# Per-head normalisation of the new vectors moved to VectorE, and their turns one step later, in a one-core decoder layer

## The reference

```python
h = rms_norm(x, attn_norm[i])
(mq, mk, mv, nsq, kc, vc, ksl, vsl, kwn, vwn, ngate, mgate) = jnp.split(h @ w_in[i], cuts, axis=-1)
q_a = rms_norm(to_heads(mq, MOBA_HEADS), moba_q_gain[i])
k_a = rms_norm(to_heads(mk, MOBA_HEADS), moba_k_gain[i])
y_a = moba_attention(q_a, k_a, to_heads(mv, MOBA_HEADS), tab_moba)
q_b = rms_norm(nsq.reshape(B, S, G, R, HEAD_DIM).transpose(0, 2, 3, 1, 4), nsa_q_gain[i])
```

## Time and profile before

| what | us |
|---|---|
| median of 3 runs (992.62 to 996.42) | 994.91 |
| the profiled execution, its own time | 993.43 |
| its span | 991.6 |
| PE busy | 913.8 (92%) |
| DVE busy | 485.4 (49%) |
| POOL busy | 381.8 (38%) |

### The profile page before, as it was taken

How to read it: one execution, slowest core, us unless ns; L and a number is a source line. 1 busy time by engine, 2 the same in 40 slices (tenths; PEclk the granted TensorE clock), 3 DMA queues, 4 the chain that set the end, 5 groups by cost and what they waited for, 6 DMA issues and landing times.

```text
span 991.6 us, 13260 instructions
## 1 busy us (share of the span) xinstructions
PE 913.8 (92%) x4581; PEld 779.1 (79%) x4581; DVE 485.4 (49%) x1145; ACT 405.8 (41%) x849; POOL 381.8 (38%) x360
## 2 busy tenths in 40 slices
PE   7898798786989889998989899999999999999988
PEld 7896688686978777877767678888888888888866
DVE  6616766767686677786431433444333342011132
ACT  5121554444454445554334354544444453232320
POOL 4723312303031211124545475444544445464540
PEclk9999899999989989999999999999999999999999
DMA  5745222214111212334554334333333333332232
GB/s 165 178 110 138 64 62 70 72 36 114 44 33 54 75 54 75 100 128 164 182 169 130 117 112 135 94 95 96 88 108 103 98 94 103 99 96 85 85 97 84
DMA packets 98917, 99.33 MB, mean 100 GB/s; under 512 B 15940, under 2 KB 73252, under 8 KB 98852
## 3 DMA queue, kind: packets, MB, share of 16 engines
q1 hardware_dynamic: 98799, 98.48, 33.9%
q10 hardware_dynamic: 53, 0.01, 0.0%
HBM read 87.58 MB, written 10.88 MB: 99 GB/s over the span
## 4 chain that ended last, share of the span: by engine, by line
PE 78%; DVE 12%; issue 4%; ACT 4%; DMA 1%; POOL 0%; SPq 0%; POOLq 0%; ACTq 0%; DVEq 0%
PE banks L1411 24%; PE banks L1413 23%; PE banks L1412 23%; DVE plain_arena L1161 2%; PE banks L1542 2%; PE banks L1460 1%; DVE plain_arena L1189 1%; DVE split_arena L1080 1%; DVE split_arena L1234 1%; PE banks L1525 1%; PE banks L1524 1%; ACT split_arena L836 1%; PE banks L1484 1%; DMA plain_arena<-in_x_dram 1%; ACT plain_arena L824 1%
## 5 line engine op out<-in xcount | busy, mean ns | idle before, releaser
L1411 PE MATMUL banks<-split_arena 128*128 128x512 f32 (+4 forms) x1224 | 471.3, 385 | 15.7 <-POOL split_arena L652 4.1
L1413 PE MATMUL banks<-split_arena 128*128 128x512 f32 (+4 forms) x1224 | 459.1, 375 | 0.0
L1412 PE MATMUL banks<-split_arena 128*128 128x512 f32 (+4 forms) x1224 | 458.6, 375 | 0.0
L652 POOL TENSOR_TENSOR split_arena<-plain_arena,split_arena 128x512 fp32r<-128x512 f32 x184 | 238.7, 1309 | 248.5 <-ACT split_arena L852 248.5
L1411 PEld LDWEIGHTS banks<-split_arena 128*128 128x128 f32 x1224 | 234.6, 192 | 58.8 <-issue 12.4
L1413 PEld LDWEIGHTS banks<-split_arena 128*128 128x128 f32 x1224 | 233.4, 191 | 36.3
L1412 PEld LDWEIGHTS banks<-split_arena 128*128 128x128 f32 x1224 | 234.5, 192 | 32.7
L852 ACT ACTIVATE split_arena<-plain_arena 128x512 fp32r<-128x512 f32 x184 | 113.3, 628 | 196.3 <-PE banks L1413 187.8
L824 ACT ACTIVATE plain_arena<-plain_arena 128x128 f32<-128x128 f32 (+1 forms) x96 | 53.9, 561 | 135.7 <-DVE plain_arena L1189 135.5
L1372 DVE SCALAR_TENSOR_TENSOR plain_arena<-banks,plain_arena 128x511 f32<-128x511 f32 x44 | 32.7, 744 | 135.3 <-ACT plain_arena L954 135.3
L620 POOL TENSOR_TENSOR split_arena<-plain_arena,split_arena 128x512 fp32r<-128x512 f32 x16 | 26.5, 1655 | 155.8 <-ACT split_arena L910 143.5
(11 more groups left out here) (158 smaller groups left out, 868.1 us busy)
## 6 DMA issues: line engine op xcount, KB each, us to landing
plain_arena<-in_w_up_dram SPq DMA_DIRECT2D x88, 256.0 KB, 3.2
plain_arena<-in_w_down_dram SPq DMA_DIRECT2D x44, 256.0 KB, 2.6
plain_arena<-in_w_in_dram SPq DMA_DIRECT2D x18, 512.0 KB, 4.4
plain_arena<-in_w_in_dram SPq DMA_DIRECT2D x32, 192.0 KB, 3.3
plain_arena<-in_x_dram SPq DMA_DIRECT2D x8, 512.0 KB, 4.7
gates<-plain_arena SPq DMA_DIRECT2D x16, 256.0 KB, 2.0
plain_arena<-skew SPq DMA_DIRECT2D x16, 256.0 KB, 3.7
plain_arena<-gates SPq DMA_DIRECT2D x16, 256.0 KB, 3.7
```

Of the source, the lines that this page charges most:

```text
L652: pool.tensor_tensor(W2l[:, c % RING, :], raw2[:, c % RING, :], W2h[:, c % RING, :].bitcast(F32), ALU.subtract).then_inc(w2_lo, 1)
L1411: nc.tensor.matmul(o, ah, bh, start=first, stop=False)
L1412: nc.tensor.matmul(o, ah, bl, start=False, stop=False)
L1413: return nc.tensor.matmul(o, al, bh, start=False, stop=last)
```

## The change

The 12 instructions of the reciprocal root are cut in two (`rsqrt_begin`: three and the first Newton round; `rsqrt_end`: the other two rounds). The first part stays at the end of the `NORM` step, the second stands in the next step between `bias` and `scale`. POOL normalises nothing more. DVE normalises all four tiles, but two vectors at a time: the even columns (half 0) behind `scale`, the odd ones (half 1) at the end of that step. `column(w, x)` is the order in which the vectors are turned. For the units 2 to 5 the turns move from the steps end+2 to end+5 to end+3, end+4, end+6 and end+7; for the units 6 and 7 the steps stay. `scores` waits for as many vectors as it needs (`vectors_needed`), no longer for all four of a pair. One semaphore, `norm_done`, counts halves.

```diff
@@ -120,7 +120,7 @@
         NORM[end], VALUES[end] = w, w
         for x in range(nvec(w)):
-            VEC[end + 2 + (w >= 6) + x] = (w, x)
+            VEC[end + 3 + x + (w < 6 and x >= 2)] = (w, x)
...
+        def column(w, x):
+
+            return {0: (0, 1, 2, 3), 5: (0, 2, 3, 1), 6: (0, 1, 2, 3), 7: (0, 2, 3, 1)}.get(w, (0, 2, 1, 3))[x]
+
+        def vectors_needed(n, k):
+
+            if n < 4:
+                return {0: 4 * n + 2, 4: 4 * n + 4}.get(k)
+            if n == 5:
+                return {0: 4 * n + 1, 9: 4 * n + 2}.get(k)
+            if n == 7:
+                return {0: 4 * n}.get(k)
+            return {0: 4 * n + 2, 4: 4 * n + 3, 9: 4 * n + 4}.get(k)
...
             def take_proj(w, tt):
...
                 if w > 1 and tt == 0:
-                    act.wait_ge(norm_dve, w)
-                    act.wait_ge(norm_done, w)
+                    act.wait_ge(norm_done, 2 * (w - 1))
...
-            def normalise(w):
+            def normalise(w, half):
...
-                for tt in range(2, NT):
-                    i = qkv[:, tt, 0:k * DH].rearrange("p (v c) -> p v c", v=k)
-                    for a in range(2):
-                        ins = nc.vector.tensor_tensor(qn[:, tt, 0:k, a * DH:(a + 1) * DH], i,
-                                                      rq[:, 4 * tt:4 * tt + k].unsqueeze(2).broadcast_to([P, k, DH]), ALU.mult)
-                ins.then_inc(norm_dve, 1)
+                r = rq[:, 0:16].rearrange("p (t v) -> p t v", t=NT)
+                i = qkv[:, :, 0:2 * P].rearrange("p t (v c) -> p t v c", v=4)
+                v = slice(half, 4, 2)
+                for a in range(2):
+                    ins = nc.vector.tensor_tensor(qn[:, :, v, a * DH:(a + 1) * DH], i[:, :, v, :],
+                                                  r[:, :, v].unsqueeze(3).broadcast_to([P, NT, 2, DH]), ALU.mult)
+                ins.then_inc(norm_done, 1)
...
                     bias(t)
+                if t - 1 in NORM:
+                    rstd_end()
                 if 1 <= t <= T:
                     scale(t - 1)
                 if t - 1 in NORM:
-                    normalise(NORM[t - 1])
+                    normalise(NORM[t - 1], 0)
...
                     if t in NORM:
-                        rstd(NORM[t])
+                        rstd_begin(NORM[t])
+                    if t - 1 in NORM:
+                        normalise(NORM[t - 1], 1)
...
-                if s["k"] == 0:
-                    pe.wait_ge(vec_lo, vec_base[min(n + 1, W_UNITS - 1)])
+                if vectors_needed(n, s["k"]):
+                    pe.wait_ge(vec_lo, vectors_needed(n, s["k"]))
```

More of the change, by code:

```diff
@@ L386, in vec_dst @@
         def vec_dst(w, x):
-            n = w - 1
+            n, x = w - 1, column(w, x)
             if w == 6:
@@ L636, in v_low @@
                     ins.then_inc(v_lo, 1)
-            def normalise(w):
-                k = nvec(w)
-                pool.wait_ge(rstd_done, w)
-                if w > 1:
-                    pool.wait_ge(vec_filled, vec_number(w - 1, nvec(w - 1) - 1))
-                for tt in range(2):
-                    i = qkv[:, tt, 0:k * DH].rearrange("p (v c) -> p v c", v=k)
-                    for a in range(2):
-                        ins = pool.tensor_tensor(qn[:, tt, 0:k, a * DH:(a + 1) * DH], i,
-                                                 rq[:, 4 * tt:4 * tt + k].unsqueeze(2).broadcast_to([P, k, DH]), ALU.mult)
-                ins.then_inc(norm_done, 1)
             def split_chunk(c):
@@ L1051, in link, with newton, rsqrt_begin @@
                 dve.wait_ge(chain, nch[0])
-            def rsqrt(dst, src, inv_n, wdt, parts=P, done=None):
-                v = st[0:parts, 40:40 + wdt]
-                y = dst
-                a = st[0:parts, 60:60 + wdt]
+            def newton(y, v, a, done=None):
+                link(nc.vector.tensor_tensor(a, y, y, ALU.mult))
+                link(nc.vector.scalar_tensor_tensor(out=a, in0=a, scalar=-0.5, in1=v, op0=ALU.mult, op1=ALU.mult))
+                ins = nc.vector.scalar_tensor_tensor(out=y, in0=a, scalar=1.5, in1=y, op0=ALU.add, op1=ALU.mult)
+                if done is not None:
+                    ins.then_inc(done, 1)
+                else:
+                    link(ins)
+            def rsqrt_begin(y, src, inv_n, wdt, parts=P):
+                v, a = st[0:parts, 40:40 + wdt], st[0:parts, 60:60 + wdt]
                 link(nc.vector.tensor_scalar(v, src, inv_n, EPS, ALU.mult, ALU.add))
@@ L1060, in rsqrt, with rsqrt_end @@
                 link(nc.vector.tensor_scalar(y.bitcast(I32), a.bitcast(I32), -1.0, float(0x5F3759DF), ALU.mult, ALU.add))
-                for it in range(3):
-                    link(nc.vector.tensor_tensor(a, y, y, ALU.mult))
-                    link(nc.vector.scalar_tensor_tensor(out=a, in0=a, scalar=-0.5, in1=v, op0=ALU.mult, op1=ALU.mult))
-                    ins = nc.vector.scalar_tensor_tensor(out=y, in0=a, scalar=1.5, in1=y, op0=ALU.add, op1=ALU.mult)
-                    if it == 2 and done is not None:
-                        ins.then_inc(done, 1)
-                    else:
-                        link(ins)
+                newton(y, v, a)
+            def rsqrt_end(y, wdt, parts=P, done=None):
+                v, a = st[0:parts, 40:40 + wdt], st[0:parts, 60:60 + wdt]
+                newton(y, v, a)
+                newton(y, v, a, done)
+            def rsqrt(y, src, inv_n, wdt, parts=P):
+                rsqrt_begin(y, src, inv_n, wdt, parts)
+                rsqrt_end(y, wdt, parts)
             def w_high(w, kts):
@@ L1236, in pt_low @@
                                             PTh[:, s["u"] % 2, 0:i + 1, P * i:P * (i + 1)].bitcast(F32), ALU.subtract).then_inc(pt_lo, 1)
-            rstd(1)
-            normalise(1)
+            rstd_begin(1)
+            rstd_end()
+            normalise(1, 0)
+            normalise(1, 1)
             vec_low(1, 0)
```

32 lines of the change are left out of this document (16 added, 16 removed).

## The result

The changed kernel takes 998.92 us (median of 11 runs, 995.6 to 1002.55); the kernel before takes 994.91 (11 runs, 992.43 to 996.46). That is slower by 4.0 us. The ratio of the executions is 1.0049 (it is not the quotient of the medians, which is 1.0040), with a 95% interval of 1.0033 to 1.0065, so that the change costs something is clear of the noise, and whether it is under or over 0.5% is not. The profiled execution is the fastest of the 11, with a span of 993.8 us.

What follows compares the result with a forecast made beforehand. PE was busy 92%, DVE 49%, so a DVE change pays only where PE waits for it. Terms +0.75 + 2.0 + 0 - 0.4 - 0.3 - 0.15 = +1.9 on 993.43 gave 995.3, as median 996 us, range 989 to 1001.

Steps and rivals of the forecast that it cites:

- The wait keeps its length: Steps 4, 12 and 20: PE idle 6.5, 3.4 and 4.1 us before a projection, until `take_proj` on ACT.
- The rival that PE gets through: Units 2 to 5: tile 0 is taken without half 1, waits of 18.1 us shrink; about 977 us, chance 0.03.
- The hold of the chain by `v_low`: POOL's `v_low` delays DVE's chain: +0.95 us each at units 2 to 4, about +2.6 at 5, +2.9 at 7.
- The rival that the chain isn't held: Units 2 to 5 and 7: `v_low` doesn't delay DVE's chain; together -6.9 us, 989 by the median, chance 0.14.
- unit 7: Held chain +2.9, product and scale -1.15, earlier `pt_low(58)` -1.2, with the rest -0.3 us.
- Unit 5: DVE is the bound; savings and the held chain leave net 0 for `scores(32)`, between -2 and +4 us.
- unit 6: `pt_low` comes 2 us earlier, but `bias(42)`, behind half 1, does not: -0.4 us.
- Net +1.0 at step 18: Moved `vec_high` and `vec_low` make `take_proj` 1.2 us later, PE comes 0.2 to 0.4 later: net +1.0 us.
- the largest term: Turns moved into steps 9 and 17: +1.0 us each at steps 10 and 18, sum +2.0, floor 0, ceiling 2 x 1.4.
- The low clock: Units 2 to 4: at two of them a turn comes out of the lower PE clock, -0.45 us each.
- The third rival: Unit 5's stretch gets longer, `scores(32)` over 4 us later relative to `scores(26)`; 1000.5 us by the median, chance 0.18.
- The sentence on the hold that would begin 0.6 us later: If the chain's first three instructions contend only in two-port mode, three units give back 0.9 us of the sum.

Runs made afterwards that it cites:

- tile_apart: The changed kernel with tile 0 of the units 3 and 5 in the staging buffer `gstage`; 988.85 us, ratio 0.9939 to the kernel before.
- tile_apart_before: The kernel before with tile 0 of the units 3 and 5 in that same staging buffer; 993.89 us, ratio 0.9995.
- turns_back: The changed kernel with its turns put back in the steps of before (4, 5, 6, 7); 995.86 us, ratio 1.001 to the kernel before.
- turns_close: The changed kernel with the turns in the steps 5, 6, 7 and 8, in unit 5 too; 1000.56 us, ratio 1.0053 to the kernel before.
- move_alone: The kernel before with only the turns of the units 2 to 5 moved as in the change; 999.39 us, ratio 1.004.
- both_back: The changed kernel with turns in the steps of before and `v_low` held until the root (units 2 to 4) or product (5, 7) is done; 989.14 us.
- values_late: The changed kernel with `v_low` held until the root (units 2 to 4) or the product (5, 7) is done; 994.87 us, ratio 1.0002 to the kernel before.

## Why the prediction was right, and where not

The forecast was 996.0 us, in a range of 989 to 1001, and no measurable change; it came to 998.92. The sum said +1.9 us, of which the profile can test 2.05 (without unit 1). It shows 4.30.

- **The wait keeps its length, and the tile's copy ends it.** Right: forecast 6.5, 3.4 and 4.1 us in the steps 4, 12 and 20, measured 6.47, 3.45 and 4.13. tile_apart and tile_apart_before show the cause: only with the copy freed and the turn moved does the wait go (to 3.02, nothing and 0.69). The rival that PE gets through was rightly excluded; it needs storage that the change didn't bring.
- **The hold of the chain by `v_low`.** Right in place and mechanism: 0.95 us forecast, 1.08 measured at unit 3, where the product's end did not move. At unit 2 it was two instructions, 0.98 and 1.19; the first was held before, too. The rival that the chain isn't held is refuted. Mis-sized at the units 5 and 7: I took 2.6 and 2.9 us, and measured 1.9, since each of the four held instructions would have run 0.17 by itself and the hold is only what exceeds that. So unit 7 gained 1.38 in the profile, where the forecast had 0.3. Two things weaken this. The terms that I named for unit 7 add up to +0.55, and "the rest", which made it -0.3, had no row behind it. And in turns_back, turns_close and tile_apart, whose unit 7 is that of the changed kernel, scores 62 to 70 took 29.36, 30.03 and 30.07 us, a gain of 1.0 down to 0.3. Unit 5 came out at -0.04 against 0, and unit 6 within -0.16 against -0.4.
- **"Net +1.0 at step 18", "at step 10 the same", "the largest term": the step that failed.** The size is near, the mechanism wrong. I said that `vec_high` and `vec_low` make `take_proj` late, and that PE would wait over 2 us for it in step 18. It waited 0.55, less than the 1.85 of the earlier trace rows, and in step 10, where I had named a wait of 1 us or more for it, there was none. In front of step 18 stood the turn's own wait of 2.14 us for bank 1, and in step 9 one of 0.75. I had followed the move on ACT and DVE, and not asked what the second turn itself waits for, although the kernel before has this wait at unit 5 (2.21 us for L1172 at 234.04, 2.16 for L1176 at 238.13). Idle time rose by 0.96 from scores 8 to 13 (1.56 less unit 3's 0.60) and by 0.99 from 13 to 20.
- **Step 25, missed.** I priced the steps 9 and 17 and took unit 4's pair of turns as free. Its second turn waits 0.75 us for the same reason; idle time rose by 0.70 (1.27 less unit 4's 0.57). The three boundaries cost 2.7 us of idle time, where I had 2.0 for two.
- **The low clock, mis-sized.** I took off 0.45 at two units, as the turn comes out of the low clock. In the profile the opposite weighs more: in scores 4 to 8 PE does 5.25 us of work at the lower of its two clocks (1.2 GHz, 0.50 in the rows) and did 2.89 before. The stretch at that clock, changed and before:

```profile
113.60:120.40 6.80, 5.25 (x18) 5.26 (x19) 2.99 (x12) 1.67 (x6) 0.00 (x0) 0.50 0.00 0
```

```profile
113.40:120.20 6.80, 2.89 (x11) 2.92 (x12) 6.03 (x13) 2.81 (x9) 3.15 (x4) 0.50 0.01 2
```

  The 2.36 us more at half speed cost 1.2 us. PE's busy time in scores 4 to 26 rose by 1.5 in all, which with the idle time (+4.3) makes the 5.84. The row of tile_apart_before above has the idle time of before and loses 1.47 us in the same stretch, so I take it for chance of one execution. That it is no term of the change was not shown.
- **The third rival**, unit 5's stretch getting over 4 us longer, did not happen.
- **The sentence on the hold that would begin 0.6 us later** has a slip: at three units that gives back 1.8 us, not 0.9. The sum doesn't use it.

For the whole time, beyond the profile's sum, the runs divide the change so: the moved turns cost 3 to 5 us (2.9 by turns_back, 4.6 by move_alone, 5.3 by both_back against values_late), `v_low` where it now stands instead of held back costs 3.9 (values_late), and the halves, the chain in two parts and POOL's rest, with `v_low` held, are worth 5.2 (both_back). Each of these numbers is uncertain by 1 to 2 us, and the parts share some of it. The time landed near the forecast partly by luck: the largest term had its size from another mechanism, and errors of both signs met: what unit 7 gained over the forecast (0 to 1.1 us, by the trace) stood against what step 25 cost.

The Trainium skill, SBUF — State Buffer, section Who interferes with whom, says that a DVE instruction with two SBUF inputs contends with GpSimd's reads, and that `tensor_scalar` can enter a two-port mode and then contends too. The traces agree: `tensor_scalar` (L1064, 1.25 us), `tensor_tensor` (L1053, 0.66) and `scalar_tensor_tensor` (L1054, 0.66) were all held. Whether `tensor_scalar` was in the two-port mode no row tells; that it was held, they do. The case that the rule might spare the chain's first three instructions did not come about.

## What to carry to other kernels

When two waits end together, removing one buys little or nothing: list all who wait for the instruction, and free the last of them in the same edit. Before moving an operation to a neighbouring step, ask what its own buffer waits for: two writers of one PSUM bank in consecutive steps are tied by the reader in between, with all that stands ahead of it in its queue. And work taken from a shared engine still has to be placed: what is left of it moves up and may meet a chain of small instructions, so it needs a time in which such a chain doesn't run beside it.

## What the runs showed of the hardware

- A held DVE instruction of 16 elements waits to about the end of POOL's: 0.98 to 1.25 us instead of 0.16 to 0.17 beside one POOL instruction of 384 or 512 elements, and 0.60 to 0.66 us each, one for one, beside four of 256. At unit 3 the one ended at 147.55 and POOL's at 147.52. In values_late scale was held for 1.1 us though its row starts 0.04 us ahead of POOL's (151.60 and 151.64).
- The same stretch of two kernels, with PE's idle time equal to 0.01 us, took 1.43 and 1.47 us more or less, with a mean granted clock of 0.93 against 1.00 and 0.80 against 0.86.
